# A mixture-of-experts encoder layer: the stores of the experts' output rows are issued by GpSimd instead of ScalarE

## The reference

```
e_idx, gw = route(uf, w_router, router_bias)      # 2 of 32 experts for each token, with weights
h = silu(xblk @ w_gate[e]) * (xblk @ w_up[e])     # w_gate, w_up: 1024 x 512
yb = h @ w_down[e]                                # 512 x 1024
y[t] = sum over the token's two experts of gw * yb
x = x + gt_ffn * y;  out = rmsnorm(x, final_g)
```

## Time and profile before

| | us |
|---|---|
| median of 3 runs | 1954.38 (1954.33 to 1954.8) |
| profiled execution, its own time | 1960.13 |
| its span | 1958.3 |
| expert loop, from 1226 to 1899 | 673 |
| busy in the span: PE / DVE / ACT / POOL | 1670.5 / 714.4 / 484.8 / 429.4 |
| DMA moved | 333.54 MB, mean 170 GB/s |

### The profile page before, as it was taken

One profiled execution on the slowest core, in us unless ns is written; L12 is line 12 of the kernel. 1 busy time (PEld: TensorE's weight loads), 2 busy tenths in 40 slices (PEclk: granted clock), 3 DMA queues, 4 the chain that ended last, 5 costly groups with the idle time before them and its releaser, 6 DMA issues.

```text
span 1958.3 us, 37977 instructions
## 1 busy us (share of the span) xinstructions
PE 1670.5 (85%) x14820; PEld 1248.8 (64%) x14820; DVE 714.4 (36%) x1304; ACT 484.8 (25%) x879; POOL 429.4 (22%) x376
## 2 busy tenths in 40 slices
PE   2889999999776999999998980998899879999970
PEld 1768777777554787777886870656656656656550
DVE  1534444445678334445225653111111111111118
ACT  1433333334645112001003100112121211121214
POOL 3312222121113333233321203111111111111112
PEclk7889999999887999999999975999999999999995
DMA  9101110100601433442115129399999999849726
GB/s 293 44 22 43 33 42 21 42 22 14 215 1 33 126 100 98 118 155 75 48 64 164 44 100 356 132 410 366 344 352 342 359 342 348 346 187 404 315 65 230
DMA packets 177650, 333.54 MB, mean 170 GB/s; under 512 B 27782, under 2 KB 102414, under 8 KB 177558
## 3 DMA queue, kind: packets, MB, share of 16 engines
q1 hardware_dynamic: 145774, 272.59, 38.5%
q10 hardware_dynamic: 21656, 29.64, 4.7%
q0 software_dynamic: 10128, 29.95, 4.4%
HBM read 302.44 MB, written 29.72 MB: 170 GB/s over the span
## 4 chain that ended last, share of the span: by engine, by line
PE 51%; DMA 27%; DVE 10%; ACT 3%; issue 2%; POOL 1%; SPq 1%; ACTq 0%; DVEq 0%; POOLq 0%
DMA d_y<-yb 23%; PE ps L708 23%; PE ps L868 6%; PE ps L893 5%; PE ps L938 4%; PE ps L784 3%; PE ps L750 3%; PE ps L948 2%; DMA w_exp<-in_w_exp_up 2%; DMA ada_g<-in_ada_w 1%; PE ps L775 1%; PE ps L834 1%; PE ps L900 1%; DVE br_lo L1416 1%; DVE br_hi L1417 1%
## 5 line engine op out<-in xcount | busy, mean ns | idle before, releaser
L938 PE MATMUL ps<-w_exp,xT 128*32 128x256 f32 x6272 | 359.8, 381 | 9.0 <-DMA w_exp<-in_w_exp_up 8.9
L708 PE MATMUL ps<-u_hi,w_hi 128*128 128x512 f32 x768 | 315.8, 411 | 16.7 <-POOL w_lo L541 16.3
L938 PEld LDWEIGHTS ps<-w_exp,xT 128*32 128x32 f32 x6272 | 254.6, 111 | 97.1 <-issue 13.0
L708 PE MATMUL ps<-u_lo,w_hi 128*128 128x512 f32 x768 | 303.5, 395 | 0.0
L708 PE MATMUL ps<-u_hi,w_lo 128*128 128x512 f32 x768 | 303.3, 395 | 0.0
L1589 DVE TENSOR_TENSOR act<-act,ps 64x256 f32<-64x256 f32 x98 | 41.6, 425 | 504.6 <-ACT act L1184 503.1
L948 PE MATMUL ps<-w_exp,actT 128*32 128x256 f32 x3136 | 204.7, 404 | 0.0
L708 PEld LDWEIGHTS ps<-u_hi,w_hi 128*128 128x128 f32 x768 | 146.6, 191 | 50.1 <-issue 24.3
L540 POOL CAST w_hi<-w_raw 128x1024 fp32r<-128x1024 f32 x48 | 54.1, 1128 | 540.4 <-PE ps L708 456.1
L708 PEld LDWEIGHTS ps<-u_hi,w_lo 128*128 128x128 f32 x768 | 146.1, 190 | 31.9
L633 POOL DMA_INDIRECT xg<-d_u,tok_cur x100 | 96.0, 960 | 311.7 <-PE ps L923 295.9
(11 more groups left out here) (255 smaller groups left out, 2192.8 us busy)
## 6 DMA issues: line engine op xcount, KB each, us to landing
w_exp<-in_w_exp_gate SPq DMA_DIRECT2D x32, 2048.0 KB
w_exp<-in_w_exp_up SPq DMA_DIRECT2D x32, 2048.0 KB
w_exp<-in_w_exp_down SPq DMA_DIRECT2D x32, 2048.0 KB
ada_g<-in_ada_w ACTq DMA_DIRECT2D x32, 512.0 KB, 3.8
d_y<-yb ACTq DMA_DIRECT2D x98, 128.0 KB
w_raw<-in_w_in SPq DMA_DIRECT2D x24, 512.0 KB, 4.1
w_raw<-in_w_branch_gate SPq DMA_DIRECT2D x24, 512.0 KB, 4.0
ada<-in_ada_w SPq DMA_DIRECT2D x4, 2048.0 KB, 15.3
```

Source lines behind the costliest of these rows:

```text
L708: ins = pe.matmul(ps[:, 5 + h, :], a[par][:, kc, :], b[:, kc, HF[h]], start=(n == 1), stop=(n == MM))
L938: last = pe.matmul(ps[CAP * n:CAP * (n + 1), 2 + h, 0:QT], x, w_exp[:, sl, off:off + QT], start=(kc == 0), stop=(kc == KC - 1))
```

## The change

POOL issues the stores, at the end of each iteration of its loop, behind the two gathers of that iteration; each waits for the evacuation of its half (`y_evac`). ScalarE keeps the copy and its wait for the store of the turn before. The zero fill is split into two DMAs of 4 MB which raise `st_y[0]` and `st_y[1]` by 16, in the place of ScalarE's starting value, and `st_pad` is gone.

```diff
-            spare = NPAIR - NE
-            pool.dma_start(d_y[NE * PAIR:, :].rearrange("(p k) (a n) -> p (k a) n", p=P, n=2 * P),
-                           zero_row[:].unsqueeze(1).to_broadcast([P, spare * PAIR * D // P // (2 * P), 2 * P])).then_inc(st_pad, 16)
+            spare = (NPAIR - NE) // 2 * PAIR
+            for h in range(2):
+
+                rows = d_y[NE * PAIR + spare * h:NE * PAIR + spare * (h + 1), :].rearrange("(p k) (a n) -> p (k a) n", p=P, n=2 * P)
+                pool.dma_start(rows, zero_row[:].unsqueeze(1).to_broadcast([P, spare * D // P // (2 * P), 2 * P])).then_inc(st_y[h], 16)
...
                 for h in range(2):
                     pool.wait_ge(xg_ps, p * 2 + h)
                     hold(pool)
                     gather_rows(h)
+                for h in range(2):
+                    pool.wait_ge(y_evac, p * 2 + (h + 2))
+                    hold(pool)
+                    rows = d_y[bass.ds(p * PAIR - PAIR + h * CAP, CAP), :].rearrange("t (n m) -> n t m", n=4)
+                    pool.dma_start(rows, yb[h][:]).then_inc(st_y[h], 16)
...
-            pool.wait_ge(st_pad, 16)
...
-            for s_, n_ in ((p_ready, PRIME), (pt_ready, PRIME), (y_ready, PRIME), (silu_ready, 1), (y_evac, 3), (st_y[0], 16), (st_y[1], 16), (mrow_ready, 1), (st_mod, 16)):
+            for s_, n_ in ((p_ready, PRIME), (pt_ready, PRIME), (y_ready, PRIME), (silu_ready, 1), (y_evac, 3), (mrow_ready, 1), (st_mod, 16)):
...
-            sc.wait_ge(st_pad, 16)
+            for h in range(2):
+                sc.wait_ge(st_y[h], 16)
...
                 sc.wait_ge(st_y[h], p * 16)
                 sc.activation(yb[h][:], ps[:, 6 + h, 0:QT], ACT.Copy).then_inc(y_evac, 1)
-                sc.wait_ge(y_evac, p * 2 + (h + 2))
-                hold(sc)
-                rows = d_y[bass.ds(p * PAIR - PAIR + h * CAP, CAP), :].rearrange("t (n m) -> n t m", n=4)
-                sc.dma_start(rows, yb[h][:]).then_inc(st_y[h], 16)
-
-            sc.wait_ge(st_pad, 16)
```

More of the change, by code:

```diff
@@ L306, in build @@
             "ld_rt", "score_ready", "hit_ready", "rank_ps", "slots_ready", "starts_ready", "st_list", "ld_list", "tok_ready"))
-        zero_set, st_pad = sem("zero_set"), sem("st_pad")
+        zero_set = sem("zero_set")
         ld_wt = {w: [sem(f"e_ld_{w}{i}") for i in range(SLOTS)] for w in "gud"}
```

## The result

The changed kernel takes 2037.8 us (median of 4 runs, 2036.4 to 2040.7), the kernel before 1954.4. The ratio is 1.0434, interval 1.0415 to 1.0452. The direction is the forecast one, and 2037.8 lies in the range; but the time rose by 83 us where 40 were forecast.

What follows compares the result with a forecast made beforehand. ScalarE's stores of `yb`, on 4 DMA engines, were taken to set the expert loop's turn. 35 turns of 15.4 us and 14 of 12.3 made 711 us against 671.3, +40 us: 1994 us, range 1938 to 2045.

Steps and rivals of the forecast that it cites:

- The start of the gathers: On GpSimd's queue behind both stores, the second gather starts 4.97 us after a turn's start, 4.0 to 6.4 at the bounds.
- The landing: From the second gather's start until its rows are there: 6.2 us beside weights, 3.0 us without.
- The tail: TensorE's time from the second half's transposes to the next turn's start: 4.2 us.
- The number of long turns: Expert-loop turns beside the weight stream: 35 of 49, at 15.4 us each.
- The rule of the forecast: Turns beside weights are the weight stream's 507 us divided by the turn's length, plus 2 the stream only touches.
- short turns: Expert-loop turns without weights in flight: 14 of 49, at 12.3 us each.
- C: Rival, much slower: GpSimd's stores on the same 4 engines with gathers behind them, turns of 17.4 us, 2044 us; chance 0.14.
- The wait of ScalarE: ScalarE's wait at the copy for the previous store of the same `yb`, 192.6 us in 39 turns, goes.
- The zero fill at nothing: Its second issue on GpSimd, at most 2.79 us, is hidden in 32.31 us of idle time.
- B: Rival, faster: with the four engines free, gathers land in 4 us beside weights, turns of 13.2 us, 1920 us; chance 0.17.
- D: Rival, same time: turns beside weights of 13.8 us, 39 of them, and some 10 us of weight stalls; chance 0.07.
- the marks named ahead: TensorE waits about 3 us for gathers in some 35 turns; store issues well over 1.5 or landings over 8 mean slower.

Runs made afterwards that it cites:

- Experiment 4: Changed kernel with only a quarter of each half's rows stored, 32 partitions instead of 128, the zero fill covering all of `d_y`: 1999.9 us, ratio 1.0242.
- experiment 5: Kernel before with ScalarE's stores in four DMAs each, GpSimd also waiting for both evacuations before index copy and gathers, issuing no store: 2001.6 us, ratio 1.0221.
- experiment 3: Changed kernel with 16 identity matmuls added in each turn ahead of TensorE's wait for the gathers: 2059.6 us in a single run.
- experiment 6: Changed kernel with 8 identity matmuls added in each turn ahead of TensorE's wait for the gathers: 2029.7 us, ratio 1.0394.
- experiment 7: Kernel before with only the zero fill cut into two DMAs of 4 MB: 1956.8 us in 10 runs, ratio 1.0008.
- experiment 1: Changed kernel with GpSimd issuing each block's stores behind the next block's gathers, so no gather stands behind an evacuation: 1888.6 us, ratio 0.9672.
- experiment 2: Kernel before with ScalarE keeping the stores, each cut into four DMAs of 32 partitions: 1906.4 us, ratio 0.9757.
- experiment 8: Changed kernel with GpSimd waiting for both evacuations, then issuing the gathers, then the two stores behind them: 1959.7 us in 10 runs, ratio 1.0018.

## Why the prediction was right in direction and short by half

**The start of the gathers: right.** Forecast 4.97 us after the product's start. Measured 6.08 - 1.17 = 4.91. The terms hold too: a store's issue took 0.74 us (0.8 taken), the first gather began 0.86 us behind the index copy and the second 1.33 behind the first (0.82 and 1.27).

**The landing: 6.2 forecast, 6.91 measured.** Here the store's size on the queue was mis-sized. The packets of 4 KB were forecast rightly, on more than 4 engines, but not the 112 small ones. By their share, q0's packets took 22.2% of 16 engines for 9 us, 2.0 us of all engines for two stores and two gathers without weights. A store takes more of the engines than a gather: before, q0 took 5.3% of 673 us for 98 gathers, 0.36 us each; after, 10.9% of 749 for 98 of both, 0.83 a pair, so a store takes 0.47. Two of them stand in front of the gathers where the forecast let nothing stand. A store lands in 7.2 us, not 6, which costs nothing by itself since `yb` is needed only a turn later. Experiment 4 takes three quarters of the stores away and gets 0.58 us back, experiment 5 has none on q0 and lands in 6.29.

**The tail: 4.2 forecast, 5.61 measured** (17.43 less 4.91 and 6.91). This is the step that failed, and the largest. "TensorE then needs from the second half's transposes ... to the next start ... 4.3 us, 4.2 without DVE's step that is long done" was read from a turn in which TensorE had not waited. The forecast itself put a wait of some 3 us in front of it, and did not ask what TensorE does after 3 us of nothing. The runs show it at 1.2 GHz behind such a wait. Experiments 3 and 6 cover the wait and bring the tail, up to the evacuation, from 4.44 to 2.70 and 3.07, where 4.2 - 1.17 = 3.03 was forecast. The Trainium skill says so in "TensorE: Matmul & The Clock Gate" (Part 1, the clock gate): an idle array drops to 1.2 GHz and returns to 2.4 once it is busy again. The trace agrees, with 0.51 from 1534.10 to 1536.50 and 1.00 behind it.

**The number of long turns: 35 forecast, 29 measured.** The rule of the forecast gives 507/17.43 + 2 = 31, so most of the difference is its divisor, the turn's length. The short turns came at 12.16 (12.3).
Together, for the differences to the forecast: start 29 x -0.1 = -3, landing 29 x 0.7 = +21, tail 29 x 1.4 = +41, six long turns fewer x 3.1 = -19, short turns 19 x -0.14 = -3: +37. With the forecast's +40 that is +77, and +79.9 were measured in the loop.

That 2037.8 lies inside the range is partly luck. Its upper part, up to 2045, stood for a second gather that starts at 6.4 with a landing of 7.0, and for C. The start was 4.9, C's engines were not the ones, and no bound was given to the tail.

**The wait of ScalarE: right**, gone in all turns, with up to 6.5 us each. **The zero fill at nothing: right** (experiment 7).

**The rivals.** B wanted gathers to land in 4 us once the 4 engines are free. They are free in experiments 1 and 2, and the median landing there is 5.8 and 5.9 us against 6.0 before: it is the weight stream that makes them late, not the stores. C named 2044 us, nearest to the result, with the wrong engines: a store alone showed 0.6 of 16 busy. That nearness is luck. Of its mechanism, gathers' packets behind stores' packets, there is 0.6 us and not 2. (B's sum has 38 turns beside weights where the forecast's rule gives 40, which changes it by 2 us.) D asked for long turns of 13.8 us; they are of 17.4. Of the marks named ahead, a wait of about 3 us came in 29 turns rather than 35; the issue stayed under 1.5; landings of the gathers had a median of 6.3 and a longest of 8.2.

What stays open: how long or how complete a wait must be before the clock falls. The traces show waits averaging 3.52 (tail 4.44, a low clock in 28 of 29 turns), 2.48 (3.66, 22 of 30), 2.26 (3.77, 22 of 29), 1.63 (3.23, 12 of 30) and hardly any (2.94 in the short turns), and single turns break the order: the one from 1737.7 waited 3.01 us and its down product took 3.66. Open too is how the 149 us between experiment 1 and the changed kernel divide without ScalarE's late stores of experiment 8. Nor was it tried whether a store could be laid out so that q0 carries it in 32 packets without the small ones.

## What to carry to other kernels

Before a DMA is moved to another queue, list what stands behind it there in program order: the wait it brings is given to all of them. The move itself was worth 3.3% as long as the gathers stayed ahead of it, and cost 4.3% when they did not. Where a forecast puts a wait in front of dense matmuls, read their duration from a place that comes behind such a wait, or add the clock's fall.

## What the runs showed of the hardware that I had not expected

- TensorE's granted clock fell to the lower level behind 3.8 us without work, for about 3.4 us, and 64 matmuls took 4.79 instead of 3.66 us. Over 29 turns the longer tail was worth 41 us against the forecast, twice what the later landing cost (21). Waits of 2.3 us on average were already followed by a low clock in 22 of 29 turns (experiment 5). In experiment 6 TensorE's idle time was no cheaper than the same time filled with useless products.
- The same 128 partitions of 1 KB go out as packets of 1 KB on 4 engines from ScalarE (13 us beside weights) and as 32 packets of 4 KB with 112 small ones, on more engines, from GpSimd (3.8 to 8.9 us). The Trainium skill ("DMA: Bandwidth & Descriptors", on why a DMA increments its semaphore by 16) lets both be, the first by its rule of the largest divisor and the second by its exception for direct copies from GpSimd; the traces agree with 4 for the one and, by the slice of 0.6, with more than 4 for the other.
- Four DMAs of 32 KB were better than one of 128 KB for the landing (at most 7.1 against 13.3 us), but the four issues took 3.05 us of ScalarE's queue in the turn shown, and with that they delayed the next evacuation and whoever waited for it.
